# A two-layer attention, convolution and mLSTM block: GpSimd's taps in tensor form, 9 of them for the last tile, the layer norm two steps ahead, two more output banks, and probability copies ahead of exponentials

## The reference, cut to what matters

```
def na_conv_mixer(h_lat, h_ctx, w_in, q_g, k_g, rpb, conv_w, conv_b, ln_g, ln_b, w_out, ctx_out):
    ...
        return q, k, heads(v), u * jax.nn.sigmoid(gt)

    def conv_module(glu):
        y = depthwise_conv(glu, conv_w, conv_b)
        return jax.nn.silu(layer_norm(y, ln_g, ln_b))
    ...
    att_lat = neighbourhood_attention(ql, kl, vl, kc, vc, rpb)
    out_lat = jnp.concatenate([att_lat, conv_module(glu_l)], axis=-1) @ w_out
```

## Time and profile before

| | |
|---|---|
| median of 3 runs | 1968.57 us (1965.87 to 1973.45) |
| profiled execution: its time, and its span | 1973.65 us, 1971.8 us |
| PE busy | 1768.8 us, 90% of the span |
| DVE busy | 844.2 us, 43% |
| ACT busy | 559.9 us, 28% |
| POOL busy | 276.9 us, 14% |
| PE's granted clock, mean | 0.921 of full speed |

### The profile page before, as it was taken

How to read it: one execution, slowest core, us unless ns; L and a number is a source line. 1 busy time by engine, 2 the same in 40 slices (tenths; PEclk the granted TensorE clock), 3 DMA queues, 4 the chain that set the end, 5 groups by cost and what they waited for, 6 DMA issues and landing times.

```text
span 1971.8 us, 26385 instructions
## 1 busy us (share of the span) xinstructions
PE 1768.8 (90%) x10440; PEld 1459.5 (74%) x10440; DVE 844.2 (43%) x1217; ACT 559.9 (28%) x901; POOL 276.9 (14%) x204
## 2 busy tenths in 40 slices
PE   5989897588999999999999468988989989999997
PEld 4877675367888888888888467666757768787886
DVE  4377686634422222222223525556545443333333
ACT  3334454242321112211222302332333232122131
POOL 0396999500000000000000000000000000000000
PEclk8999898689999999999999759898869999999999
DMA  7623332022113421233215301001002323323333
GB/s 301 76 75 108 101 125 97 1 86 64 44 63 105 148 89 63 59 138 134 63 64 192 120 0 43 22 33 32 22 11 75 128 75 96 95 88 94 96 96 106
DMA packets 47314, 168.99 MB, mean 86 GB/s; under 512 B 5392, under 2 KB 5648, under 8 KB 47120
## 3 DMA queue, kind: packets, MB, share of 16 engines
q1 hardware_dynamic: 31408, 115.47, 18.4%
q10 hardware_dynamic: 15072, 51.53, 7.3%
q0 software_dynamic: 768, 1.08, 0.7%
HBM read 163.83 MB, written 4.19 MB: 85 GB/s over the span
## 4 chain that ended last, share of the span: by engine, by line
PE 78%; DVE 8%; POOL 6%; ACT 3%; issue 2%; DMA 2%; SPq 0%; ACTq 0%; DVEq 0%; POOLq 0%
PE PS L445 57%; PE PS L1643 5%; POOL X L392 3%; PE PS L1537 3%; POOL X L394 2%; PE PS L1546 2%; PE PS L1767 2%; PE PS L1869 2%; DMA scr<-in_ada 2%; PE PS L1868 1%; DVE scr L1416 1%; PE PS L1843 1%; PE PS L1597 1%; DVE w_lo L430 1%; DVE h_lo L963 1%
## 5 line engine op out<-in xcount | busy, mean ns | idle before, releaser
L445 PE MATMUL PS<-h_hi,w_hi 128*128 128x512 f32 (+1 forms) x1296 | 401.0, 364 | 3.7 <-DVE w_lo L430 3.2
L445 PE MATMUL PS<-h_lo,w_hi 128*128 128x512 f32 (+1 forms) x1296 | 394.0, 358 | 0.0
L445 PE MATMUL PS<-h_hi,w_lo 128*128 128x512 f32 (+1 forms) x1296 | 393.8, 358 | 0.0
L430 DVE TENSOR_TENSOR w_lo<-raw,w_hi 128x1024 fp32r<-128x1024 f32 x196 | 240.9, 1231 | 280.3 <-ACT w_hi L425 267.3
L425 ACT ACTIVATE w_hi<-raw 128x1024 fp32r<-128x1024 f32 x196 | 206.2, 1052 | 299.5 <-PE PS L445 244.1
L445 PEld LDWEIGHTS PS<-h_hi,w_hi 128*128 128x128 f32 x1296 | 217.7, 192 | 47.8 <-DVE w_lo L430 5.6
L445 PEld LDWEIGHTS PS<-h_lo,w_hi 128*128 128x128 f32 x1296 | 216.8, 191 | 37.1
L445 PEld LDWEIGHTS PS<-h_hi,w_lo 128*128 128x128 f32 x1296 | 215.5, 190 | 37.3
L445 PE MATMUL PS<-c_hi,w_hi 128*128 128x512 f32 (+1 forms) x688 | 215.9, 367 | 24.7 <-DVE c_lo L1009 18.7
L445 PE MATMUL PS<-c_lo,w_hi 128*128 128x512 f32 (+1 forms) x688 | 213.4, 363 | 0.0
L445 PE MATMUL PS<-c_hi,w_lo 128*128 128x512 f32 (+1 forms) x688 | 212.4, 362 | 0.0
(11 more groups left out here) (259 smaller groups left out, 2055.6 us busy)
## 6 DMA issues: line engine op xcount, KB each, us to landing
raw<-in_w SPq DMA_DIRECT2D x196, 512.0 KB, 3.4
scr<-in_ada ACTq DMA_DIRECT2D x48, 512.0 KB, 5.7
adaw<-in_ada ACTq DMA_DIRECT2D x32, 512.0 KB, 4.3
scr<-in_ada SPq DMA_DIRECT2D x8, 1024.0 KB, 10.6
X<-in_xT SPq DMA_DIRECT2D x4, 768.0 KB, 6.8
X<-in_xT ACTq DMA_DIRECT2D x1, 3072.0 KB, 9.9
x_spill<-X ACTq DMA_DIRECT2D x1, 2048.0 KB, 9.3
X<-x_spill ACTq DMA_DIRECT2D x1, 2048.0 KB, 8.6
```

The costliest lines, as they stand in the source:

```text
L430: nc.vector.tensor_tensor(w_lo[:, j], raw[:, j].rearrange("p (k n) -> p k n", k=KT), w_hi[:, j].bitcast(f32), ALU.subtract).then_inc(s_lo, 1)
L445: last = nc.tensor.matmul(G[j][:, a:b], w[:, j, k], m[:, k, a:b], start=(n == 1), stop=(n == 3 * k_tiles))
```

## The change

Five things are changed.

1. POOL's multiplies are no longer a TENSOR_SCALAR with the weight as a scalar operand, but a TENSOR_TENSOR whose second input is the weight's column, broadcast along the 798 columns. The adds stay.
2. POOL takes 9 taps of the last tile instead of 13, and DVE 22 instead of 18 (`POOL_TAPS`, `DVE_TAPS`). DVE's taps per step (`TAPS_AT`) become 5, 5, 4, 4, 4 in steps 12 to 16 instead of 3 each in steps 12 to 17, and the last merge stands after step 16 instead of 18.
3. The layer norm's parts move up: channel sums in step 17, centring in steps 17 and 18, squares in 18 and 19, their sums in step 20, the reciprocal root in step 20, products in steps 21 and 22. The load of X moves from step 21 to step 19, and the load of SiLU's table behind the loop.
4. The outputs of `attend` in steps 18 to 22 go to banks 2 and 3 in turn, and the transposes of these steps no longer wait for `attn_lo` of the step before; `attend(U)` waits for that of step U-2.
5. On ACT, up to step 15, the probability copies of tile U stand ahead of the exponentials of tile U+1. In steps 16 to 23 the old order stays.

```diff
-POOL_TAPS = 13
-DVE_TAPS = TAPS - POOL_TAPS
-POOL_OPS = 2 * POOL_TAPS - 1
+POOL_TAPS = (13, 13, 13, 9)
+DVE_TAPS = tuple(TAPS - n for n in POOL_TAPS)
+DVE_DONE = tuple(sum(DVE_TAPS[:i + 1]) for i in range(4))
+POOL_DONE = tuple(sum(2 * n - 1 for n in POOL_TAPS[:i + 1]) for i in range(4))
...
+TAIL = 17
...
-                        nc.gpsimd.tensor_scalar(y2, src[:, tap:tap + SPAN], w, None, ALU.mult).then_inc(s_pc, 1)
+                        nc.gpsimd.tensor_tensor(y2, src[:, tap:tap + SPAN], w.to_broadcast([128, SPAN]), ALU.mult).then_inc(s_pc, 1)
...
-                    nc.gpsimd.tensor_scalar(ptmp, src[:, tap:tap + SPAN], w, None, ALU.mult).then_inc(s_pc, 1)
+                    nc.gpsimd.tensor_tensor(ptmp, src[:, tap:tap + SPAN], w.to_broadcast([128, SPAN]), ALU.mult).then_inc(s_pc, 1)
...
-        OT = PS[:, 6, 0:128]
+        OT = [PS[:, 6 if U < TAIL or U == NU - 1 else 2 + U % 2, 0:128] for U in range(NU)]
...
+                if U <= 15:
+                    probs_out(U)
                 if U + 1 < NU:
                     exponentials(U + 1)
-                probs_out(U)
+                if U > 15:
+                    probs_out(U)
...
-                if U in (20, 21):
-                    for i in range(2 * U - 40, 2 * U - 38):
+                if U in (18, 19):
+                    for i in range(2 * U - 36, 2 * U - 34):
...
-                if U == 21:
+                if U == 19:
                     act.wait_ge(s_mrg, 4)
                     act.wait_ge(s_sc, 8)
                     act.dma_start(X[:], A["xT"]).then_inc(s_x, 16)
-                if U == 22:
+                if U == 20:
                     act.wait_ge(s_lns, 2)
-                    nc.scalar.activation(lnm, SSR, ACT.Ln, scale=1.0 / 512, bias=eps[:]).then_inc(s_lna, 1)
+                    nc.scalar.activation(lnm, PSf[:, 0:T], ACT.Ln, scale=1.0 / 512, bias=eps[:]).then_inc(s_lna, 1)
...
-                    nc.scalar.preload_act_table(ACT.Silu)
+            nc.scalar.preload_act_table(ACT.Silu)
...
-            TAPS_AT = (4, 4) + 16 * (3,)
+            TAPS_AT = (4, 4) + 10 * (3,) + (5, 5, 4, 4, 4)
...
-                if U in (20, 21):
-                    ln_centre(U - 18)
...
-                if U in (2, 7, 12, 18):
-                    merge((2, 7, 12, 18).index(U))
-                if U == 19:
+                if U in (2, 7, 12, 16):
+                    merge((2, 7, 12, 16).index(U))
+                if U in (17, 18):
                     dve.wait_ge(s_lns, 1)
-                    ln_centre(0)
-                    ln_centre(1)
+                    ln_centre(2 * U - 34)
+                    ln_centre(2 * U - 33)
...
-                if U == 23:
+                if U in (21, 22):
                     dve.wait_ge(s_lna, 2)
                     dve.wait_ge(s_lnp, 8)
-                    for i in range(4):
+                    for i in range(2 * U - 42, 2 * U - 40):
...
+                pe.wait_ge(s_alo, NU - 1)
...
-                    elif U:
+                    elif U and U <= TAIL:
                         pe.wait_ge(s_alo, U)
...
                 pe.wait_ge(s_PT, U + 1)
+                if U > TAIL:
+                    pe.wait_ge(s_alo, U - 1)
...
-                if U == 19:
+                if U == 17:
                     pe.wait_ge(s_mrg, 4)
...
-                if U == 22:
+                if U == 20:
+                    pe.wait_ge(s_lnd, 8)
                     for i in range(4):
                         pe.wait_ge(s_lnp, 2 * i + 2)
```

More of the change, by code:

```diff
@@ L381, in pool_conv @@
                 for j in range(j0, j1):
-                    tap = DVE_TAPS + j
+                    tap = DVE_TAPS[i] + j
                     w = sm("conv_w", TAPS * i + tap)
@@ L397, in _ @@
             masks(0)
-            pool_conv(0, 0, POOL_TAPS)
+            pool_conv(0, 0, POOL_TAPS[0])
             pool_conv(1, 0, 6)
             masks(1)
-            pool_conv(1, 6, POOL_TAPS)
+            pool_conv(1, 6, POOL_TAPS[1])
             pool_conv(2, 0, 4)
             masks(2)
-            pool_conv(2, 4, POOL_TAPS)
+            pool_conv(2, 4, POOL_TAPS[2])
             pool_conv(3, 0, 4)
             masks(3)
-            pool_conv(3, 4, POOL_TAPS)
+            pool_conv(3, 4, POOL_TAPS[3])
             pool.wait_ge(s_g2, GD_END)
@@ L483, in attn_views @@
                 dst = c[:, hp, 0:LAT].rearrange("p (r t c) -> p t c r", r=ROWS, t=4)[:, t]
-                return dst, OT.rearrange("p (c r) -> p c r", c=16)
-            return c[:, hp, LAT + 128 * (t - 4):LAT + 128 * (t - 3)], OT
+                return dst, OT[U].rearrange("p (c r) -> p c r", c=16)
+            return c[:, hp, LAT + 128 * (t - 4):LAT + 128 * (t - 3)], OT[U]
         def keys(U):
@@ L1115, in conv_steps @@
                 for _ in range(n):
-                    i, j = cs[0] // DVE_TAPS, cs[0] % DVE_TAPS
+                    i = next(i for i in range(4) if cs[0] < DVE_DONE[i])
+                    j = cs[0] - (DVE_DONE[i] - DVE_TAPS[i])
                     y, src, w = convy[i], glus[i % 2][:, j:j + SPAN], sm("conv_w", TAPS * i + j)
@@ L1127, in merge @@
             def merge(i):
-                assert cs[0] >= DVE_TAPS * (i + 1)
-                dve.wait_ge(s_conv, DVE_TAPS * (i + 1))
-                dve.wait_ge(s_pc, POOL_OPS * (i + 1))
+                assert cs[0] >= DVE_DONE[i]
+                dve.wait_ge(s_conv, DVE_DONE[i])
+                dve.wait_ge(s_pc, POOL_DONE[i])
                 V.tensor_tensor(convy[i], convy[i], y2, ALU.add).then_inc(s_mrg, 1)
@@ L1140, in glu_out @@
                 if i >= 2:
-                    dve.wait_ge(s_conv, DVE_TAPS * (i - 1))
-                    dve.wait_ge(s_pc, POOL_OPS * (i - 1))
+                    dve.wait_ge(s_conv, DVE_DONE[i - 2])
+                    dve.wait_ge(s_pc, POOL_DONE[i - 2])
                 V.tensor_tensor(dst[:, 15:15 + LAT], g[:, 0:LAT], sgm[:, 0:LAT], ALU.mult)
@@ L1696, in attend @@
                         f = 128 * hp + 64 * h
-                        last = MM(OT[64 * h:64 * h + 64], Vt[0:size, VSLOT[b], f:f + 64],
+                        last = MM(OT[U][64 * h:64 * h + 64], Vt[0:size, VSLOT[b], f:f + 64],
                                   PTs[0:size, h, 128 * n:128 * n + 128], start=(n == 0), stop=(n == len(blocks) - 1))
@@ L1737, in _ @@
                         for a, b in BOTH:
-                            last = MM(SSR[:, a:b], ones, lnt[:, i, a:b], start=(i == 0), stop=(i == 3))
+                            last = MM(PSf[:, a:b], ones, lnt[:, i, a:b], start=(i == 0), stop=(i == 3))
                     last.then_inc(s_lns, 1)
```

7 lines of the change are left out of this document (2 added, 5 removed).

## The result

The changed kernel takes 1979.39 us at the median of 20 runs (1970.36 to 1987.33). The kernel before, timed beside it, takes 1972.92 us over 20 runs. The ratio is 1.0037, with a 95% interval from 1.0025 to 1.0049: the change makes the kernel some 6.5 us **slower**, where 32 us less were forecast.

The account below looks back on a forecast made before the run. POOL's stream of taps was taken as the bound from 245 to 373 us. Last merge -39.9, tail +8.1, sum -31.8; with 1 us before step 0 about -32, giving 1937 us (forecast 1933 to 1941, range 1929 to 1949).

Parts of the forecast that it names:

- steps 7 to 11: Step 7 takes 10.3 us, 1 us is allowed at merge 1, steps 8 to 11 take 43.1; step 12 starts at 279.6.
- steps 12 to 16, to the merge's end: DVE is the bound: 53.3 us busy, 1.1 us of waits; last merge ends at 334, 39.9 us earlier.
- The price of a tap on POOL: POOL's new multiply takes 1.60 us instead of 2.28; a multiply-and-add pair takes 3.85 us instead of 4.5.
- rival 2: POOL's multiplies: tensor form no cheaper (2.28 us); four exchanged pairs save 18 us there; 10 to 12 saved, 1957; chance 0.05.
- rival 4: POOL's multiplies in tiles 1 to 3: broadcast weight read anew for each column; at 3.5 us each, 1989 us; chance 0.03.
- I keep the 0.45 a pair: A multiply and add on POOL beside DVE's work take 0.45 us more than undisturbed, as in tile 1 before.
- rival 1: POOL stays the bound in tiles 1 to 3, disturbed by 0.75 us a pair; 26 us saved, 1943; chance 0.17.
- shorter POOL instructions should also shorten DVE's waits: Taps ahead of step 0, beside tile 0: DVE waits less for POOL, counted as 1 us gained.
- Step 5, copies first: 9.5 us less: PE no longer waits for the masks in step 5, which takes 9.4 us instead of 18.9; step 6 starts at 213.9.
- Balance of POOL and DVE: Four taps of the last tile cost 5 us on DVE, 15.4 on POOL; DVE bounds steps 12 to 16, POOL 2 us off.
- From the last merge to the projection: Seven light steps instead of five take 43.8 us, 8.1 more than 35.7; the new banks costed at nothing.
- All later stages unchanged: Behind the output projection, dense PE work without tie to POOL comes 32 us earlier at unchanged length.

Follow-up runs that it names:

- Experiment 1: A small kernel of its own, POOL and DVE instructions alone and side by side: DVE's tap takes 1.05 us alone, 2.41 beside POOL's add.
- experiment 2: The kernel before with only POOL's multiplies changed to tensor form: 1985.09 us, ratio 1.0070 to the kernel before.
- experiment 10: The kernel of experiment 6 with POOL's multiplies in tensor form: 1971.92 us, ratio 1.0001 to the kernel before.
- experiment 3: The changed kernel with POOL's multiplies back in scalar form: 1967.96 us, ratio 0.9977 to the kernel before.
- Experiment 11: The kernel of experiment 6 with step 5's modulation row and low half ahead of DVE's last two taps: 1952.35 us, ratio 0.9914 to the kernel before.
- experiment 4: The kernel before with only the probability copies ahead of the exponentials up to step 15: 1966.39 us, ratio 0.9969 to the kernel before.
- experiment 8: The kernel of experiment 3 with the old order on ACT, exponentials first, in every step: 1971.76 us, ratio 1.0000 to the kernel before.
- experiment 5: The kernel of experiment 3 with probability copies first in all 24 steps: 1960.44 us, ratio 0.9939 to the kernel before.
- experiment 7: The kernel of experiment 5 with all outputs of attend in bank 6 again and the earlier waits: 1966.07 us, ratio 0.9971 to the kernel before.
- experiment 6: The kernel of experiment 5 with 12 and 8 taps of the last two tiles on POOL: 1953.93 us, ratio 0.9905 to the kernel before.
- experiment 9: The kernel of experiment 6 with two of tile 0's taps moved from DVE to POOL: 1951.77 us, ratio 0.9913 to the kernel before.

## Why the prediction was wrong

The projection was forecast at 377.8 and starts at 416.9, 39.1 us later. By the prediction's own steps:

| piece | forecast | measured | late, us |
|---|---|---|---|
| up to step 5 (before: 204.5) | 204.5 | 215.2 | 10.7 |
| steps 5 and 6 | 9.4 + 11.3 | 9.3 + 20.1 | 8.7 |
| steps 7 to 11 | 54.4 | 56.4 | 2.0 |
| steps 12 to 16, to the merge's end | 54.4 | 69.3 | 14.9 |
| merge to projection | 43.8 | 46.6 | 2.8 |

(Steps begin where PE issues the scores of the next tile: 215.17, 224.44, 244.53 and 300.98 for steps 5, 6, 7 and 12.)

**"The price of a tap on POOL" failed, in what the two engines cost each other.** Its first half was right: 1.60 us was forecast for the multiply undisturbed, 1.51 was measured, so rivals 2 and 4 fell. Its second half, "I keep the 0.45 a pair" and 1.24 us for DVE's tap, carried over numbers from a kernel in which more than half of POOL's tap time was the scalar multiply. Experiment 1 shows a tap at 1.32 us beside that multiply, at 2.41 beside the add and at 2.09 beside the new multiply. In tensor form there is nothing left that DVE can run beside cheaply. A pair lost 0.91 us at the mean, not 0.45. No rival priced this either: rival 1 let POOL pay for the disturbance, none let DVE pay.

Ahead of step 0 this cost 11.6 us in the changed kernel's profiled execution, where "shorter POOL instructions should also shorten DVE's waits" gave 1 us of gain; the same edit cost 7.0 in experiment 2 and 8.6 in experiment 10. In steps 12 to 16 DVE's taps took 36.96 us, not 26.0. Two of these 23 taps (4.3 us) belong to step 11: DVE came out of it that much later than PE, where the forecast let both begin together. The 21 that were reckoned with took 32.63 us, 1.55 each for 1.24. The rest of DVE's work was 26.2 us for 27.3, and its idle time 6.1 for 1.1; that makes up the 14.9. The edit was priced on the engine that runs it, and most of its bill came on the other one.

Experiments 2, 3 and 10 put a size on it: 12, 11 and 18 us of the whole time, in three surroundings, with the projection 7.5, 17.4 and 17.2 us later in the profiled executions. The sign of the result hangs on this edit: without it the change is 5 us faster than before. But it is not the whole miss: of the 39.1 us by which the projection came late, 21.7 stay in scalar form (399.5 against 377.8), of which the next paragraph has a part.

The page "SBUF — State Buffer" (Who interferes with whom) of the Trainium skill, cited in the prediction, has two SBUF inputs on DVE and a GpSimd instruction that reads SBUF exclude each other. The small kernel of experiment 1 agrees for POOL's add and broadcast multiply, to within 0.4 us a pair, and for an accumulator in PSUM, which frees DVE. It differs for POOL's scalar multiply, which reads SBUF as well and costs the tap 0.27 us. So the rule alone would not have given the sign: by it the old multiply (2.28 us) would hold DVE longer than the new one (1.51), and the edit would gain on both engines. That was rival B of experiment 1. The prediction saw the rule confirmed in two maxima, did not ask which of POOL's two instructions had caused them, and took the mean of 1.24 as the price beside all.

**"Step 5, copies first: 9.5 us less" failed too.** Step 5 itself came out as forecast (9.3 us for 9.4). But step 6 took 20.1 for 11.3, since the transposes of tile 6 wait for the modulation row, a wait that the prediction did not list: it asked when tile 6's probabilities would be ready, and not what else stands on DVE behind the maximum. Experiment 11 shows the link, and experiment 4 that scalar form has the same stall. Steps 5 and 6 together took 30.2 us before and 29.4 after, where 20.7 were forecast.

**Balance of POOL and DVE: right in direction.** POOL left the chain and DVE became the bound, by far more than forecast: POOL waits 45.1 us for merges. In scalar form POOL stays the bound (experiment 3), as rival 1 had it, and the exchange of four pairs moves the last merge 13.8 us with the old order on ACT (experiment 8) and 18.5 with the changed one (experiment 3), near the 18 of rival 2. Rival 2's price for the form was wrong, but its kernel, in which the multiply gives no gain, is about what experiment 3 built: 10.1 us gained at the projection, 5 in the median, for its 10 to 12.

**From the last merge to the projection: right,** 43.8 for 46.6, and not by luck: no step is more than 1.1 us off. The largest are step 23, and step 20, where a row was misread: the sums of squares took 6.22 us before at a mean clock of 0.84, not at half the full clock, so 3.1 was too little for them.

```profile
398.20:404.50 6.30, 6.30 (x19) 3.27 (x19) 0.78 (x3) 1.27 (x5) 0.00 (x0) 0.84 0.96 410
```

```profile
397.10:402.40 5.30, 5.30 (x20) 2.90 (x18) 1.02 (x4) 2.32 (x5) 0.00 (x0) 1.00 0.99 424
```

(Before, and after: they took 5.33 us there.) No run takes the banks alone in the order that the change keeps in the last steps, so that they are worth nothing there is not shown. With copies first there they are worth 5.6 us (experiments 5 and 7), which the prediction's reason, "the exponentials of U+1 still stand ahead of the copies", allows for: remove that, and the low half is next.

**All later stages unchanged:** right within the spread of single executions.

The version that came out best is the change's own plan in scalar form, with copies first everywhere and 12 and 8 taps: 1951.8 to 1953.9 us (experiments 6, 9 and 11), 1.3% less than the changed kernel and 0.9% less than the kernel before.

## What to carry to other kernels

Price an instruction by what runs beside it as well: before giving GpSimd a faster form, ask whether the old one was what VectorE could run beside, and measure the mean on both engines (a median can hide it: it is 1.48 us for the tap in experiment 10, and 2.18 in the changed kernel). When an engine's order is changed to pass a stall, list every result that stands on the stalled engine behind it; the next of them takes its place, as it did twice here. A stall on a busy engine need not be on the path: taking away 6.5 us of PE's wait in one step brought nothing where POOL and DVE set the end; 6.2 us of it came back two steps later.
